# Four later modulation sections as multiply-and-sum work on VectorE, Pool and ScalarE instead of TensorE products

## The chip, the core and the metric

The kernel runs on one core of one Trainium2 chip. The metric is the device time of one execution in microseconds (us). Lower is better.

## The reference

Two requests (`prompt` and `sample`, called groups 0 and 1) go through the same two layers. Each layer begins with a modulation that is computed from the request's condition vector `c`:

```python
for l in range(DEPTH):                                   # DEPTH = 2, D_MODEL = 1024, SEQ = 512
    mod = jax.nn.silu(c) @ w_ada[l] + b_ada[l]           # (1, 1024) @ (1024, 3072)
    shift, scale, gate = jnp.split(mod, 3, axis=-1)
    h = rmsnorm(x, g_norm[l]) * (1 + scale[:, None, :]) + shift[:, None, :]
    out = even_mixer(h, ...) if l % 2 == 0 else odd_mixer(h, ...)
    x = x + gate[:, None, :] * out
return rmsnorm(x, g_final)
```

`even_mixer` starts with one input projection, `u = h @ w_in0`, whose columns go to the two kinds of attention and a SiLU gate. The modulation has six sections of 1024 values: shift, scale and gate of layer 0 and of layer 1. Shift and scale of layer 0 are needed before the first projection. The other four are needed later: the gate of layer 0 after the first output projection, those of layer 1 in the second layer.

## The kernel before

Activations lie transposed, feature by token: a tile is 128 features by T = 512 tokens, and D = 1024 is DC = 8 such tiles. One program runs a prologue (`p_*`) and then, for each group, a first layer (`a_*` is the input projection, then `b_*`, `c_*`, `d_*`) and a second layer (`e_*`). Each engine has its own hand-written sequence of instructions; they meet only through counting semaphores, and each engine works strictly in its order. All loads and stores are issued from SyncE (SP).

**The blocks.** The weights of all projections come as 81 blocks of 128 output features per group. Block b of the first in-projection (b = 0 to 24) is 8 x 3 matmuls of 128x512 (`pe_project`, `three`, L561 to L563), because each f32 operand is split into a high and a low part. For each block ScalarE makes the high half of the weights (`act_split`, L531) and VectorE the low half (`dve_split`, L543). There are PAIRS = 2 buffers of split weights and SLOTS = 3 of loaded ones (`stream_weights`, L556). ScalarE and VectorE split block b+2 in their turn b, after block b's result has been taken out of PSUM. TensorE waits for `w_lo` before each block. Block 16 is narrow (L629, 16 matmuls).

**VectorE's turn b** in `a_vector`: evict or finish block b (L832, L842, L849, L852; at b = 15 also four norms of the latents, L837), then `dve_split(b + 2)`. **Pool**, in group 0, adds masks to eight attention bias tables (L761, two instructions each) and sums the squares of the latents (L741); SP loads and stores those tables at odd b from 5. TensorE needs the sums of squares before block 9.

**The later modulation sections before.** Three passes p of TensorE compute 16 each of the 48 tiles of the modulation (6 sections x 8): pass 0 in the prologue, passes 1 and 2 in the in-projection of group 0. A pass has 8 steps, one for each 128 rows of the weights. After the block b of the table `ADA_AT` stands one `ada_step` (L303): four products of the 128x2 silu(c) with 128x512 weights, each into its own quarter of the output partitions. `ada_load` (L296) fetches the next 2 x 512 KB once the step has read the last. `ada_evict` (L319), `ada_turn` (L311, four transposes) and `ada_add` (L328) bring the sums into `mod`.

```python
ADA_AT = {b: s for s, b in enumerate((1, 3, 4, 6, 7, 9, 10, 12, 14, 15, 17, 18, 20, 21, 22, 23))}
...
for q in range(4):
    if p:
        pe.wait_ge(sem(f"ada_in{q // 2}"), 16 * (DC * (p - 1) + k + 1))
    last = pe.matmul(ps(ADA_BANK[p])[32 * q:32 * q + G], siluc[:, G * k:G * k + G], parts[q],
                     start=(k == 0), stop=(k == DC - 1))
```

After block 24 comes `b_*`, the up-projections of the latents: ScalarE takes out the first results at L947, VectorE starts at L973 after the last store of the gate (`sg_out`), Pool copies at L1004, and TensorE's first attention score is L1115.

## Time and profile before

| | |
|---|---|
| median of three runs | 1488.36 us (1488.08 to 1489.69) |
| the profiled execution, its own time | 1488.46 us |
| its span, first to last instruction | 1486.4 us |
| TensorE matmul busy | 1449.8 us, 98% of the span |
| VectorE, ScalarE, Pool busy | 854.4, 669.9, 365.2 us |
| mean granted TensorE clock | 0.997 |

The profile is one execution on the chip. "Busy" of TensorE is the union of pipelined matmuls. The in-projection of group 0 lies between 40 and 201 us of the span. The profile's chain of waits goes back from the last instruction to what released it. "Releaser" names what an engine's idle time waited for. Idle time of an engine that nobody waits for costs nothing.

### The profile page before, as it was taken

What the parts mean: (1) busy time and instruction counts of PE and PEld (TensorE: products, weight loads), DVE (VectorE), ACT (ScalarE), POOL (GpSimd) and SP (SyncE); (2) the same over time, 40 slices, a digit from 0 to 9 for tenths busy, and PEclk for the clock granted to TensorE, in tenths of its full rate; (3) what the DMA queues carried; (4) which work ended last, traced back from release to release, by engine and by line L of the source; (5) the groups of instructions that cost most, each with busy time, mean ns of one, the idle gap of its engine ahead of it and who ended that gap; (6) DMA issues with size and microseconds to landing.
All of it is one profiled execution on the core that took longest, in us unless ns stands there. A gap on an engine that the chain in (4) does not pass through costs nothing.

```text
span 1486.4 us, 18893 instructions
## 1 busy us (share of the span) xinstructions
PE 1449.8 (98%) x7162; PEld 1115.2 (75%) x7162; DVE 854.4 (57%) x1523; ACT 669.9 (45%) x1161; POOL 365.2 (25%) x455
## 2 busy tenths in 40 slices
PE   8999999999999999999999999999999999999997
PEld 5677765678787787787888887567878778787885
DVE  7523345655797427885443434566689652789423
ACT  3323446744443435543543343765444343555332
POOL 2011023421100022765210002342120002376311
PEclk9999999999999999999999999999999999999999
DMA  9566732214333331116334544222433333111531
GB/s 385 203 221 214 256 128 86 58 57 142 107 99 100 95 111 57 44 29 240 88 97 160 133 119 111 96 58 58 142 111 100 95 107 106 50 43 31 183 99 71
DMA packets 54618, 174.27 MB, mean 117 GB/s; under 512 B 6000, under 2 KB 7408, under 8 KB 52224
## 3 DMA queue, kind: packets, MB, share of 16 engines
q1 hardware_dynamic: 54528, 173.07, 36.0%
q8 instruction: 57, 0.93, 0.3%
q14 instruction: 33, 0.27, 0.1%
HBM read 149.94 MB, written 23.10 MB: 116 GB/s over the span
## 4 chain that ended last, share of the span: by engine, by line
PE 82%; DVE 8%; ACT 4%; DMA 2%; issue 2%; POOL 1%; SPq 0%; DVEq 0%; ACTq 0%; POOLq 0%
PE ps L561 21%; PE ps L563 21%; PE ps L562 21%; PE ps L1115 3%; PE ps L1151 2%; PE ps L1170 2%; PE ps L1658 1%; PE ps L1641 1%; DVE w_lo L543 1%; PE ps L303 1%; PE ps L1692 1%; PE ps L1189 1%; PE ps L1482 1%; PE ps L1132 1%; DMA at<-z_kept 1%
## 5 line engine op out<-in xcount | busy, mean ns | idle before, releaser
L543 DVE TENSOR_TENSOR w_lo<-at,w_hi 128x1024 fp32r<-128x1024 f32 x160 | 199.1, 1244 | 345.2 <-ACT w_hi L531 345.1
L531 ACT ACTIVATE w_hi<-at 128x1024 fp32r<-128x1024 f32 x162 | 169.5, 1047 | 140.1 <-PE ps L563 130.6
L561 PE MATMUL ps<-h_e_hi,w_hi 128*128 128x512 f32 x464 | 182.8, 394 | 5.0 <-DVE w_lo L543 5.0
L563 PE MATMUL ps<-h_e_hi,w_lo 128*128 128x512 f32 x464 | 180.6, 389 | 0.0
L562 PE MATMUL ps<-h_e_lo,w_hi 128*128 128x512 f32 x464 | 180.6, 389 | 0.0
L561 PE MATMUL ps<-h_a_hi,w_hi 128*128 128x512 f32 x384 | 153.7, 400 | 1.6 <-DVE h_a_lo L593 1.0
L562 PE MATMUL ps<-h_a_lo,w_hi 128*128 128x512 f32 x384 | 150.1, 391 | 0.0
L563 PE MATMUL ps<-h_a_hi,w_lo 128*128 128x512 f32 x384 | 150.0, 391 | 0.0
L561 PEld LDWEIGHTS ps<-h_e_hi,w_hi 128*128 128x128 f32 x464 | 87.1, 188 | 28.8 <-issue 8.7
L563 PEld LDWEIGHTS ps<-h_e_hi,w_lo 128*128 128x128 f32 x464 | 87.1, 188 | 18.3
L562 PEld LDWEIGHTS ps<-h_e_lo,w_hi 128*128 128x128 f32 x464 | 87.1, 188 | 18.0 <-issue 0.5
L1300 POOL TENSOR_SCALAR at<-at,at 128x256 f32<-128x256 f32 (+1 forms) x128 | 76.0, 611 | 98.9 <-DVE at L1250 98.9
L561 PE MATMUL ps<-u_h_hi,w_hi 128*128 128x512 f32 x256 | 100.2, 391 | 0.0
L563 PE MATMUL ps<-u_h_hi,w_lo 128*128 128x512 f32 x256 | 99.6, 389 | 0.0
L562 PE MATMUL ps<-u_h_lo,w_hi 128*128 128x512 f32 x256 | 99.6, 389 | 0.0
L1468 DVE SCALAR_TENSOR_TENSOR at<-ps,at,at 128x510 f32<-128x510 f32 (+1 forms) x128 | 95.9, 749 | 4.5
L561 PEld LDWEIGHTS ps<-h_a_hi,w_hi 128*128 128x128 f32 x384 | 72.4, 188 | 29.8 <-issue 12.0
L1569 POOL TENSOR_TENSOR at<-at,at 128x512 f32<-128x512 f32 x16 | 22.2, 1412 | 284.9 <-DMA at<-a_rows 284.9
L563 PEld LDWEIGHTS ps<-h_a_hi,w_lo 128*128 128x128 f32 x384 | 72.4, 188 | 15.4
L562 PEld LDWEIGHTS ps<-h_a_lo,w_hi 128*128 128x128 f32 x384 | 72.5, 189 | 14.8 <-issue 0.7
L573 POOL TENSOR_TENSOR at<-at,at 128x512 f32<-128x512 f32 x25 | 38.1, 1525 | 138.1 <-ACT at L1895 95.0
L1234 DVE TENSOR_REDUCE at<-ps 128x2 f32<-128x1024 f32 x32 | 39.2, 1225 | 42.8 <-PE ps L1115 42.8
(289 smaller groups left out, 3007.0 us busy)
## 6 DMA issues: line engine op xcount, KB each, us to landing
at<-blocks_in SPq DMA_DIRECT2D x162, 512.0 KB, 3.8
at<-w_ada SPq DMA_DIRECT2D x32, 512.0 KB, 4.6
at<-w_ada SPq DMA_DIRECT2D x8, 1024.0 KB, 17.7
at<-xs SPq DMA_DIRECT2D x4, 2048.0 KB, 10.7
z_kept<-at SPq DMA_DIRECT2D x32, 256.0 KB, 2.1
at<-z_kept SPq DMA_DIRECT2D x32, 256.0 KB, 2.7
sg_kept<-at SPq DMA_DIRECT2D x16, 256.0 KB, 4.5
at<-sg_kept SPq DMA_DIRECT2D x16, 256.0 KB, 2.6
```

The costliest lines, as they stand in the source:

```text
L531: act.activation(whi[:, n % PAIRS, :, cols], wring[:, n % SLOTS, :, cols], ACT.Copy).then_inc(sem("w_hi"), 1)
L543: dve.tensor_tensor(wlo[:, n % PAIRS], wring[:, n % SLOTS], whi[:, n % PAIRS].bitcast(F32), ALU.subtract)\
L561: pe.matmul(o, stationary[0], moving[0], start=first, stop=False)
L562: pe.matmul(o, stationary[0], moving[1], start=False, stop=False)
L563: return pe.matmul(o, stationary[1], moving[0], start=False, stop=final)
L573: pool.tensor_tensor(acc, acc, sqb[:, c % 2], ALU.add).then_inc(sem("sq_added"), 1)
L1115: last = pe.matmul(ps(s_bank(j) + e), qcat[0:QK, u, m * P:(m + 1) * P], kcat[0:QK, u], start=True, stop=True)
L1151: last = pe.transpose(ps(4 + q)[:, col:col + P], Pt[:, j % 4, m, k * P:(k + 1) * P], ident)
L1170: last = pe.matmul(ps(6 + n % 2)[64 * e:64 * e + 64, 2 * P * half:2 * P * half + 2 * P], vmla[:, s, 2 * n + e], PT[(j - 1 + e) % 4][:, 2 * ...
L1234: dve.tensor_reduce(nmx[:, 2 * i:2 * i + 2], ps2(i % 2).rearrange("p (e t) -> p e t", e=2), AX.X, ALU.max, negate=True).then_inc(sem("c_ma ...
L1300: last = pool.tensor_scalar(p, p, rinv[:, n:n + 1], 1.0, ALU.mult, ALU.mult)
L1468: dve.scalar_tensor_tensor(y[:, lo:hi], src[:, lo + d:hi + d], vb("convw", t * IC + c), y[:, lo:hi], ALU.mult, ALU.add).then_inc(sem("e_co ...
```

## The change

The four later sections leave TensorE in the in-projection of group 0. The weights of these sections are given transposed (`w_late`): a tile `w_late[t]` is 128 output features by the 1024 inputs, and `srep[g]` holds c of group g, broadcast from memory to all 128 partitions and put through SiLU once by ScalarE (both c in ScalarE's turn 0). A value of `mod` is then the sum over a row of `w_late[t] * srep[g]`.

- 24 tiles (gate of layer 0, shift and scale of layer 1) are done by VectorE, two instructions for each (`late_column`, one per group, each with a sum output), one tile in most turns b: the first instruction ahead of `dve_split`, the second behind it. None stands at b = 16, two at b = 14. Tiles 0 to 15 use two buffers in turn, tiles 16 to 23 one buffer; the load of the next waits until the last reader of its buffer is done.
- 8 tiles (gate of layer 1) are multiplied by Pool (`gate_products`, one instruction of 128x1024 per group) and summed by ScalarE (`gate_sums`) in turns b = 3, 5, ... 17; SP loads the next one (`gate_load`) after both sums of the last.
- The bias is added in `late_section` or `late_bias`. ScalarE's part of `b_*` begins with a wait for all nine increments of `mod_set`.
- The loads are 32 of 512 KB, as many bytes as before, and two of 512 KB for `srep`.
- The buffer `navT` of group 0 lies elsewhere.

```diff
-    ada_q = [take(2 * T, at=V0 + n * T) for n in (2, 9)]
+    late_w = [take(D, at=V0 + 2 * T), take(D, at=xT_lo)]
+    late_g = take(D, at=xT_lo + 2 * T)
+    late_p = take(D, at=xT_lo + 4 * T)
+    srep = [take(D, at=V0 + 9 * T), take(D, at=htmp_lo)]
+    unread = take(2 * (acc_lo - rstd_lo), at=rstd_lo).rearrange("p (h w) -> p h w", h=2)[:, :, 0:T]
...
+    LATE = 3 * DC
+    LATE_AT = [b for b in range(1, 25) for _ in range(0 if b == 16 else 2 if b == 14 else 1)]
+    ONE_SLOT = 16
+    MOD_SET = 9
...
+    def late_load(sp, t):
+
+        uses = late_uses(t)
+        if len(uses) > 1:
+            sp.wait_ge(sem("late_col"), G * (uses[-2] + 1))
+        sp.dma_start(late_w[late_slot(t)], w_late[t]).then_inc(sem(f"ada_in{late_slot(t)}"), 16)
+
+    def late_column(dve, t, g):
+
+        if g == 0:
+            dve.wait_ge(sem(f"ada_in{late_slot(t)}"), 16 * (1 + len(late_uses(t))))
+        if t == 0:
+            dve.wait_ge(sem("p_silu"), g + 2)
+        if t or g:
+            dve.wait_ge(sem("late_col"), G * t + g)
+        l, c = divmod(2 * DC + t, 3 * DC)
+        w = late_w[late_slot(t)].rearrange("p (h w) -> p h w", h=2)
+        dve.scalar_tensor_tensor(w if g else unread, w, 1.0, srep[g].rearrange("p (h w) -> p h w", h=2), ALU.mult, ALU.mult,
+                                 accum_out=mod[:, l, c, g:g + 1]).then_inc(sem("late_col"), 1)
...
+    def gate_load(sp, k):
+
+        if k:
+            sp.wait_ge(sem("late_sum"), G * k)
+        sp.dma_start(late_g, w_late[LATE + k]).then_inc(sem("ada_in2"), 16)
+
+    def gate_products(pool, k):
+
+        if k == 0:
+            pool.wait_ge(sem("p_silu"), 1 + G)
+        pool.wait_ge(sem("ada_in2"), 16 * (k + 2))
+        if k:
+            pool.wait_ge(sem("late_sum"), G * k)
+        for g in range(G):
+            if g:
+                pool.wait_ge(sem("late_prod"), G * k + g)
+            pool.tensor_tensor(late_g if g else late_p, late_g, srep[g], ALU.mult).then_inc(sem("late_prod"), 1)
+
+    def gate_sums(act, k):
+
+        for g in range(G):
+            act.wait_ge(sem("late_prod"), G * k + g + 1)
+            o = late_g if g else late_p
+            act.activation(o, o, ACT.Copy, accum_out=mod[:, 1, 2 * DC + k, g:g + 1]).then_inc(sem("late_sum"), 1)
...
-        ada_load(sp, 0)
+        sp.wait_ge(sem("ada_used"), 4)
+        late_load(sp, 0)
+        sp.dma_start(srep[0], c_in[0:1, :].to_broadcast([P, D])).then_inc(sem("ada_in3"), 16)
...
-                if g == 0 and b in ADA_AT and ADA_AT[b] + 1 < ADA_STEPS:
-                    ada_load(sp, ADA_AT[b] + 1)
+                if g == 0:
+                    for t in range(1, LATE):
+                        if max(LATE_AT[t] - 1, 1) == b:
+                            if t == 1:
+                                sp.wait_ge(sem("h_lo"), DC)
+                                sp.dma_start(srep[1], c_in[1:2, :].to_broadcast([P, D])).then_inc(sem("ada_in4"), 16)
+                            late_load(sp, t)
+                    if b % 2 and b // 2 < DC:
+                        gate_load(sp, b // 2)
                 stream_weights(sp, b + 1)
...
+            for k in range(2):
+                gate_products(pool, k)
...
+                if h + 2 < DC:
+                    gate_products(pool, h + 2)
+            pool.wait_ge(sem("late_sum"), G * DC)
+            late_bias(pool, 1, 2 * DC)
...
-                if g == 0:
-                    if b in ADA_AT:
-                        ada_step(pe, 1 + ADA_AT[b] // DC, ADA_AT[b] % DC,
-                                 [ada_q[q // 2][:, q % 2 * T:(q % 2 + 1) * T] for q in range(4)])
-                    if b == B_NAV + 1:
-                        pe.wait_ge(sem("lat_ln"), at("lat_ln", 2))
-                        ada_turn(pe, 1)
-                    if b == B_OUT0 - 1:
-                        ada_turn(pe, 2)
...
+                todo = [t for t in range(LATE) if LATE_AT[t] == b] if g == 0 else []
+                for t in todo[:1]:
+                    late_column(dve, t, 0)
                 dve_split(dve, b + PAIRS)
+                for t in todo:
+                    if t > todo[0]:
+                        late_column(dve, t, 0)
+                    late_column(dve, t, 1)
+                    if (t + 1) % DC == 0:
+                        late_section(dve, t)
...
+                if g == 0 and b == 0:
+                    for n in range(G):
+                        act.wait_ge(sem(f"ada_in{3 + n}"), 32)
+                        act.activation(srep[n], srep[n], ACT.Silu).then_inc(sem("p_silu"), 1)
+                if g == 0 and b >= 3 and b % 2 and (b - 3) // 2 < DC:
+                    gate_sums(act, (b - 3) // 2)
...
-                            act.wait_ge(sem("h_scaled"), DC)
+                            act.wait_ge(sem("late_col"), G * ONE_SLOT)
                         act.wait_ge(sem("lat_ready"), at("lat_ready", 4))
+                    if g == 0 and b == B_GATE + 1:
+                        act.wait_ge(sem("late_sum"), G * DC)
...
         def b_scalar(act):
+            if g == 0:
+                act.wait_ge(sem("mod_set"), MOD_SET)```

The order on ScalarE around turns 0 to 3 of the in-projection, before (`at_3072_66` is the ring of loaded weights, `at_2048_81` the latents):

```order
L898 ACTIVATE at_2048_81<-ps 128x512 [waits blk_done]
L531 ACTIVATE w_hi<-at_3072_66 128x1024 [waits blk_done,w_in2]
L531 ACTIVATE w_hi<-at_3072_66 128x1024 [waits blk_done,w_in0]
L898 ACTIVATE at_2048_81<-ps 128x512 [waits blk_done]
L531 ACTIVATE w_hi<-at_3072_66 128x1024 [waits blk_done,w_in1]
L531 ACTIVATE w_hi<-at_3072_66 128x1024 [waits blk_done,w_in2]
```

and in the changed kernel, where `at_1024_120` and `at_1024_121` are `srep[0]` and `srep[1]`, and `at_1024_119` and `at_1024_118` are `late_p` and `late_g`:

```order
L963 ACTIVATE at_2048_81<-ps 128x512 [waits blk_done]
L590 ACTIVATE w_hi<-at_3072_66 128x1024 [waits blk_done,w_in2]
L991 ACT_TABLE_LOAD
L991 ACTIVATE at_1024_120<-at_1024_120 128x1024 [waits ada_in3]
L991 ACTIVATE at_1024_121<-at_1024_121 128x1024 [waits ada_in4]
L590 ACTIVATE w_hi<-at_3072_66 128x1024 [waits blk_done,w_in0]
L963 ACTIVATE at_2048_81<-ps 128x512 [waits blk_done]
L590 ACTIVATE w_hi<-at_3072_66 128x1024 [waits blk_done,w_in1]
L590 ACTIVATE w_hi<-at_3072_66 128x1024 [waits blk_done,w_in2]
L362 ACTIVATE at_1024_119,at_96_52<-at_1024_119 128x1024 [waits late_prod]
L362 ACTIVATE at_1024_118,at_96_52<-at_1024_118 128x1024 [waits late_prod]
```

The two SiLUs stand between the splits of blocks 2 and 3; the second waits for the load of `srep[1]`.

The order on SP at its turn 1, in the changed kernel (`at_1024_121` is `srep[1]`, `at_1024_117` and `at_1024_116` the two buffers of VectorE's tiles, `at_1024_118` Pool's buffer):

```order
L759 DMA at_1536_79<-up_q 128x1536 [waits p_fold]
L760 DMA at_2048_82<-up_kv 128x2048
L787 DMA at_1024_121<-c_in 128x1024 [waits h_lo]
L302 DMA at_1024_117<-w_late 128x1024
L343 DMA at_1024_118<-w_late 128x1024
L615 DMA at_3072_66<-blocks_in 128x1024 [waits w_lo]
```

Before, two loads of `w_ada` stood at the place of the three from `c_in` and `w_late`.

The order on VectorE in turn 4, before:

```order
L849 SCALAR_TENSOR_TENSOR naq_lo<-ps,naq_hi 128x128 [waits naqk_hi]
L849 SCALAR_TENSOR_TENSOR naq_lo<-ps,naq_hi 128x128 x2
L849 SCALAR_TENSOR_TENSOR naq_lo<-ps,naq_hi 128x8x8 x2
L543 TENSOR_TENSOR w_lo<-at_3072_66,w_hi 128x1024 [waits w_hi]
```

and in the changed kernel (`at_96_52` is `mod`, `at_15360_122` the output that nobody reads):

```order
L914 SCALAR_TENSOR_TENSOR naq_lo<-ps,naq_hi 128x128 [waits naqk_hi]
L914 SCALAR_TENSOR_TENSOR naq_lo<-ps,naq_hi 128x128 x2
L914 SCALAR_TENSOR_TENSOR naq_lo<-ps,naq_hi 128x8x8 x2
L314 SCALAR_TENSOR_TENSOR at_15360_122,at_96_52<-at_1024_117,at_1024_120 128x2x512 [waits late_col,ada_in1]
L602 TENSOR_TENSOR w_lo<-at_3072_66,w_hi 128x1024 [waits w_hi]
L314 SCALAR_TENSOR_TENSOR at_1024_117,at_96_52<-at_1024_117,at_1024_121 128x1024 [waits late_col]
```

One instruction over two tiles of SBUF now stands on either side of the split.

## Rows read from the trace of the kernel before

**Rows 1.** The page: busy us (share of the span) x instructions.
```profile
PE 1449.8 (98%) x7162; PEld 1115.2 (75%) x7162; DVE 854.4 (57%) x1523; ACT 669.9 (45%) x1161; POOL 365.2 (25%) x455
```
**Rows 2.** Busy us, blocks 3 to 16: PE, PEld, DVE, ACT, POOL; clock, DMA share, GB/s.
```profile
59.50:148.80 89.30, 89.30 (x427) 63.86 (x425) 28.55 (x47) 26.59 (x41) 11.51 (x14) 1.00 0.68 231
```
**Rows 3.** Timeline of TensorE: start us, us, operation [idle before <-releaser].
```profile
64.57 0.39 PE L562 MATMUL ps<-h_a_lo,w_hi 128*128 128x512 f32 x1
64.80 0.39 PE L563 MATMUL ps<-h_a_hi,w_lo 128*128 128x512 f32 x1
65.12 1.04 PE L303 MATMUL ps<-at,at 128*2 128x512 f32 x8
...
66.43 0.40 PE L562 MATMUL ps<-h_a_lo,w_hi 128*128 128x512 f32 x1
```
**Rows 4.** The same timeline: the steps or turns that are not like that.
```profile
54.06 0.47 PE L561 MATMUL ps<-h_a_hi,w_hi 128*128 128x512 f32 x1 [0.65 <-DVE w_lo L543]
...
71.75 1.31 PE L303 MATMUL ps<-at,at 128*2 128x512 f32 x8
...
186.39 2.17 PE L303 MATMUL ps<-at,at 128*2 128x512 f32 x8
...
200.70 0.60 PE L311 MATMUL ps<-at,at 128*128 128x128 f32 x4
```
**Rows 5.** DMA issues between 54.6 and 56.3 us: KB each, median us to landing.
```profile
at<-up_kv SPq DMA_DIRECT2D x1, 1024.0 KB, 7.2
at<-w_ada SPq DMA_DIRECT2D x2, 512.0 KB, 8.4
```
**Rows 6.** Timeline of SP: when those loads of `w_ada` were issued.
```profile
55.26 1.03 SPq L296 DMA_DIRECT2D at<-w_ada  x2
```
**Rows 7.** Timeline of VectorE and Pool where both use two tiles of SBUF.
```profile
328.10 0.75 DVE L1356 SCALAR_TENSOR_TENSOR y_e_lo<-at,at,y_e_hi 128x512 fp32r<-128x512 f32 x1
328.14 1.86 POOL L573 TENSOR_TENSOR at<-at,at 128x512 f32<-128x512 f32 x1 [3.58 <-ACT at L1369]
333.54 1.87 DVE L1356 SCALAR_TENSOR_TENSOR y_e_lo<-at,at,y_e_hi 128x512 fp32r<-128x512 f32 x1
333.58 1.29 POOL L573 TENSOR_TENSOR at<-at,at 128x512 f32<-128x512 f32 x1 [3.58 <-ACT at L1369]
```
**Rows 8.** Groups by line and shape: names, shapes xcount | busy us, mean ns.
```profile
L1966 DVE DVE_READ_ACCUMULATOR at<-ps,at 128x1 f32 x64 | 5.2, 82 | 0.0
L531 ACT ACTIVATE w_hi<-at 128x1024 fp32r<-128x1024 f32 x162 | 169.5, 1047 | 140.1 <-PE ps L563 130.6
L543 DVE TENSOR_TENSOR w_lo<-at,w_hi 128x1024 fp32r<-128x1024 f32 x13 | 16.1, 1242 | 12.3 <-ACT w_hi L531 12.3
L837 DVE SCALAR_TENSOR_TENSOR at<-at,at,at 128x512 f32<-128x512 f32 x4 | 2.7, 744 | 0.0
L741 POOL TENSOR_TENSOR at<-at 128x512 f32<-128x512 f32 x2 | 2.5, 1280 | 0.0
L761 POOL TENSOR_TENSOR at<-at,at 128x256 f32<-128x256 f32 x16 | 12.1, 775 | 133.5 <-DMA t_masked<-at 77.9 <-DMA at<-rpb_pad 55.6
```
**Rows 9.** DMA issues at 81 us: one load of a block alone in the queue.
```profile
at<-blocks_in SPq DMA_DIRECT2D x1, 512.0 KB, 3.5
```
**Rows 10.** Stretch behind the prologue (clock 0.50), and TensorE's timeline there.
```profile
40.00:41.00 1.00, 1.00 (x3) 0.70 (x3) 1.00 (x2) 0.00 (x0) 0.00 (x0) 0.50 0.78 320
...
39.61 0.76 PE L561 MATMUL ps<-h_a_hi,w_hi 128*128 128x512 f32 x1 [0.98 <-DVE h_a_lo L593]
...
42.31 0.45 PE L561 MATMUL ps<-h_a_hi,w_hi 128*128 128x512 f32 x1
```
**Rows 11.** Timeline behind block 24 (started at 195.12): VectorE, Pool, TensorE.
```profile
208.61 0.68 DVE L973 TENSOR_TENSOR at<-ps,at 32x512 f32<-32x512 f32 x1 [4.54 <-DMA sg_kept<-at]
211.84 5.78 POOL L1004 COPY at<-at 32x512 f32<-32x512 f32 x7 [0.68 <-DVE at L977]
220.72 1.88 PE L1115 MATMUL ps<-at,at 96*128 96x512 f32 x4
```

More of the change, by code:

```diff
@@ L81, in out1_block, with trunk @@
     return 4 * quad + n % 4, n // 4
-def trunk(nc, xs, rows_in, fold_in, w_ada, blocks_in, up_q, up_kv, rpb_pad, const_in, out):
+def trunk(nc, xs, rows_in, c_in, fold_in, w_ada, w_late, blocks_in, up_q, up_kv, rpb_pad, const_in, out):
     a_rows = nc.dram_tensor("a_rows", (2 * ML_H, T), F32, kind="Internal").ap()
@@ L392, in p_tensor @@
         for k in range(DC):
[L393 to L394 removed]
+            pe.wait_ge(sem(f"ada_in{k}"), 16)
+            ada_step(pe, k)
             if k == 5:
@@ L2268 @@
     out = nc.dram_tensor("out", (G, D, T), F32, kind="ExternalOutput").ap()
-    trunk(nc, t["xs"], t["rows_in"], t["fold_in"], t["w_ada"], t["blocks_in"], t["up_q"], t["up_kv"], t["rpb_pad"], t["const_in"], out)
+    trunk(nc, t["xs"], t["rows_in"], t["c_in"], t["fold_in"], t["w_ada"], t["w_late"], t["blocks_in"], t["up_q"], t["up_kv"], t["rpb_pad"], t["const_in"], out)
     r = run_bass_kernel_spmd(nc, [arrays], core_ids=[0])
```

109 lines of the change are left out of this document (50 added, 59 removed).

## The prediction

> **What bounds the kernel now.** I read the page first: TensorE is busy for 98% of the span [rows 1]. So what leaves TensorE is worth its full price, provided that nothing makes TensorE wait. The busy time by stretch says the same of the place of the change: from block 3 to block 16 TensorE is busy for all of 89.3 us, at full clock (2.4 GHz), while VectorE has 28.55 us of work, ScalarE 26.59 and Pool 11.51 [rows 2]. By busy time alone there is room for all that is moved. What has to be asked is when each piece runs and what waits behind it.
>
> **What is removed.** The timeline of TensorE shows the price of one step. In a block, matmuls start every 0.23 us (64.57, 64.80). Around a step the last L563 starts at 64.80 and the second matmul of the next block at 66.43, 1.63 us where two intervals are 0.45: a step costs 1.18 us [rows 3]. There are 16, but the one behind block 1 is free: block 2 then still waits 0.65 us for `w_lo` [rows 4], and will without it. 15 x 1.18 = 17.7. Two steps took longer for their weights: 1.31 us where others take 1.04, which is 0.3 more, and 2.17, 1.1 more [rows 3, 4]. The last turn took 0.5 (L311 at 200.70, 0.60 long, with the next product started at 201.23), and the other about as much. Sum removed: 17.7 + 0.3 + 1.1 + 1.0 = **20.1 us**.
>
> **The second SiLU, in front of the split of block 3.** ScalarE cannot split block 3 before `srep[1]` is there. SP issues that load in its turn 1 behind `up_q` and `up_kv`, where the first `w_ada` load went out at 55.26 [rows 6]. `up_kv`, issued at 54.8, landed after 7.2 us, and the two `w_ada` loads behind it after 8.4 in the median [rows 5], so `srep[1]` lands near 63.6. Then come the SiLU (1.05, taken from L531, which has its shape), the high half (1.05) and the low half (1.24) [rows 8]: block 3 starts at 67.0. It started at 59.5 before [rows 2]. Nothing stands in between that TensorE could do. **+7.5 us.** Between 4 (the load overtakes part of `up_kv`) and 9 (128 reads of one row are slow).
>
> **VectorE and Pool, blocks 3 to 16.** The timeline shows that the two exclude each other when both work on two tiles of SBUF. A Pool product of 512 takes 1.29 us alone, and 1.86 when VectorE's L1356 had begun 0.04 us earlier; the same L1356 takes 0.75, and 1.87 when Pool got in first [rows 7]. Each time the loser waits for the winner's whole instruction (0.75 - 0.18, and 1.29 - 0.17). The Trainium skill (SBUF — State Buffer, SBUF: two separate sides) calls it an exclusive lock held for a whole instruction, which speaks against putting such work on both engines at once; the trace agrees (0.57 and 1.12 us of waiting). New instructions of this kind are 48 columns on VectorE and 16 products on Pool. What needs the pair between the starts of block 3 and block 17 [rows 8]:
> - 16 Pool products of 1024, two of 512 each: L741's two took 2.5, so 16 x 2.5 = 40.0
> - 31 columns (tiles 0 to 15, less the very first) at the price of L543, 1.24: 38.4
> - 13 splits of full width 16.1, the narrow one about 0.4
> - 14 of L761's 16, each of half a 512 at 0.64: 9.0; its mean of 775 ns includes waiting
> - L741 2.5, L837 2.7.
>
> That is 109 us. TensorE's own work there is 89.3 less nine steps (10.6), less 0.3 and 0.5: 78.0. The pair is asked for 31 us more than TensorE needs. The last tile's two products (5 us) may fall behind block 17, and the pair stands idle while Pool waits for a load and VectorE for ScalarE. These two about cancel. **+30 us**, from 15 (if much of Pool's work slips into the later blocks) to 40 (if the idle time is larger: each round of Pool is load, two products, two sums, and SP, on which the block loads hang too, waits for the sums). Where the stall shows: TensorE waits for `w_lo`, because a product stands before a split or a column.
>
> **One buffer, blocks 17 to 24.** From tile 17 on the load waits for the last reader. A round is: landing of 512 KB 3.5 [rows 9] with 0.1 to issue, two columns and one split 3 x 1.24, two reads of the sum 0.08 each [rows 8]: 7.5 us. A block is 24 x 0.227 = 5.4. So from where VectorE's slack of some 3 us is used up, each block waits 2.1. The slack lasts until block 20, and the last two tiles hold no block of this projection. Blocks 21 to 24 wait: 4 x 2.1, less what is left of the slack, **+7.5** (4 to 12; the store of the gate and the block loads can delay a landing).
>
> **Behind block 24.** VectorE ends the last section some 16.6 us after block 24 starts, since tiles 22 and 23 each need another round. ScalarE waits for it before its first eviction. In the kernel before, Pool's copies, before the first score, ended at 217.6, and the score started at 220.7, so 3 us of slack lie there. VectorE's start hangs on the last store [rows 11], which now goes out behind the split of block 26, near 19.2 us after the start of block 24 where it was 13.5 (208.61 less 195.12), 5.7 later. 5.7 less 3 gives **+3** (1 to 7).
>
> **Clock.** Behind the prologue's small matmuls the granted clock was 0.50, that is 1.2 GHz, and six matmuls took 2.70 us (39.61 to 42.31) in place of 1.36 [rows 10]. No row shows a gap in full blocks, so each of the gaps (one of 7.5 us, some eight of 2 to 7) costs between 0 and 1.35; part of it is covered, since the pair and not TensorE sets the end. **+3** (0 to 10). The Trainium skill, TensorE: Matmul & The Clock Gate, Why this matters for your kernels, says to avoid idle gaps in the middle of a kernel for this reason; by it nearly every long gap would cost the full 1.35, and the sum would be about 5 us higher.
>
> ScalarE's sums (16 of some 1.2 us) and its wait for Pool are inside the third term. The loads carry the same bytes: no term.
>
> **Sum.** -20.1 + 7.5 + 30 + 7.5 + 3 + 3 = +30.9 on the execution's 1488.46, 1519.4. The median is 0.1 lower: **1519 us**. Its own range is 1503 to 1534.
>
> **The rivals.**
> - *The pair costs about half*: Pool's products run mostly while VectorE evicts from PSUM or waits. For: VectorE is idle for long in the trace of before. Against: the sum of 109 counts only what excludes. The third term is 10 to 15: about 1502.
> - *The round of Pool is the longer one*: load 3.5, two products 5, waits for the lock up to 2 x 1.24, two sums 2.4, with SP's block loads behind it: 13.4 for two blocks (10.9), and VectorE waits on top. The third term is 50: 1540.
> - *The pair costs nothing*, and the two loops and the SiLU remain: -20.1 + 7.5 + 7.5 + 3 + 1.4 = -0.7, 1488. Rows 7 are against it.
> - *Faster*: the work hides as its busy time suggests. The mechanism is that TensorE gets its 20.1 us back because VectorE always has the low half ready. It needs no exclusion, and a round of the single buffer under 5.4 us, that is a landing under 1.5 us in place of 3.5. Then only the SiLU (7.5) and 2 are left: 1478. Against it: rows 7 and 9.
>
> **Chances.** My forecast 0.70, half the pair's cost 0.10, the longer round 0.10, no cost of the pair 0.05, faster 0.05. The range of 1500 to 1535 holds the forecast's own range and most of the half-cost case. About 0.2% (3 us) is what a measurement of this kernel can tell from no change. Faster by more than that 0.05, within it 0.05, slower 0.90.
>
> **What would show it.** In the profile after: no L303 after 50 us; TensorE's wait before block 3 near 7.5 us, released by the split; Pool products of 2.5 us alone and up to 3.7 behind VectorE, with splits and columns stretched up to 3.7; TensorE waiting for `w_lo` between blocks 4 and 17 for about 30 us in all; block starts 7.5 us apart from block 20; VectorE waiting for `w_late` there; stretches at clock 0.50 in the in-projection. I am wrong if products and columns keep their short durations side by side, or if block 3 starts before 63 us.

## The result, and the profile after

The changed kernel takes **1519.18 us** (median of four runs, 1515.15 to 1519.66), the one before 1488.44 (1488.08 to 1489.69): ratio 1.0197, with a 95% interval of 1.0184 to 1.0209. It is 30.7 us slower. The forecast was 1519. The profiled execution took 1519.66, its span is 1517.8.

The busy line of the page of the changed kernel, which answers to [rows 1]:

```profile
PE 1446.2 (95%) x7026; PEld 1120.8 (74%) x7026; DVE 942.8 (62%) x1618; ACT 689.4 (45%) x1196; POOL 421.7 (28%) x472
```

TensorE has 136 matmuls fewer and is busy for only 3.6 us less, since part of them runs at the lower clock. VectorE gained 88 us of busy time and Pool 56, for work that takes some 59 and 40 us at the lone prices of [rows 7, 8]. (A lone price is what an instruction takes when the other engine is idle.)

The waits of TensorE in the in-projection of the changed kernel, in its timeline (start us, us, operation, idle time in front and who ended it):

```profile
66.76 0.79 PE L620 MATMUL ps<-h_a_hi,w_hi 128*128 128x512 f32 x1 [7.07 <-DVE w_lo L602]
92.93 0.47 PE L620 MATMUL ps<-h_a_hi,w_hi 128*128 128x512 f32 x1 [1.57 <-DVE w_lo L602]
101.86 0.47 PE L620 MATMUL ps<-h_a_hi,w_hi 128*128 128x512 f32 x1 [3.22 <-DVE w_lo L602]
...
163.38 1.09 PE L847 MATMUL ps<-at,at 128*128 128x128 f32 x4 [6.27 <-DVE at L907]
165.61 0.79 PE L620 MATMUL ps<-h_a_hi,w_hi 128*128 128x512 f32 x1 [1.14 <-DVE w_lo L602]
192.50 0.47 PE L620 MATMUL ps<-h_a_hi,w_hi 128*128 128x512 f32 x1 [2.26 <-DVE w_lo L602]
200.00 0.47 PE L620 MATMUL ps<-h_a_hi,w_hi 128*128 128x512 f32 x1 [1.80 <-DVE w_lo L602]
207.44 0.47 PE L620 MATMUL ps<-h_a_hi,w_hi 128*128 128x512 f32 x1 [1.75 <-DVE w_lo L602]
214.81 0.47 PE L620 MATMUL ps<-h_a_hi,w_hi 128*128 128x512 f32 x1 [1.69 <-DVE w_lo L602]
...
231.99 1.47 PE L1098 MATMUL ps<-at,at 128*128 128x512 f32 x2 [2.06 <-ACT at L1022]
```

The first row is block 3 behind the second SiLU. The next ones, with two smaller ones left out, are the pair, VectorE and Pool holding each other up. At 163.38 the token transposes in front of block 17 wait 6.3 us for one eviction of VectorE. The last four block rows are blocks 21 to 24, 7.4 to 7.5 us apart, where a block is 5.44 us of work.

Why that eviction is late stands in the timelines of VectorE and Pool of the changed kernel:

```profile
154.88 7.80 DVE L902 SCALAR_TENSOR_TENSOR at<-at,at,at 128x512 f32<-128x512 f32 x4
162.60 0.68 DVE L907 COPY at<-ps 128x512 f32<-128x512 f32 x1
...
153.78 6.19 POOL L355 TENSOR_TENSOR at<-at,at 128x1024 f32<-128x1024 f32 x2 [4.43 <-DMA at<-w_late]
159.94 2.20 POOL L831 TENSOR_TENSOR at<-at,at 128x256 f32<-128x256 f32 x2
```

Four norms that take 2.7 us alone [rows 8] take 7.80 beside two products and a mask of Pool, and the copy that TensorE needs is queued behind them. Pool's products stretch too: 6.19 for two that take 5.0 alone. This is the exclusion of [rows 7], in the place where it costs most.

The same stretches by engine, in columns as in [rows 2]: blocks 3 to 16, blocks 17 to 23, and from block 24 to the first score.

```profile
66.76:165.61 98.85, 84.74 (x348) 66.07 (x348) 93.75 (x107) 43.03 (x71) 61.79 (x29) 0.93 0.64 208
165.61:214.81 49.20, 41.70 (x168) 33.16 (x169) 33.11 (x41) 17.84 (x27) 8.97 (x7) 0.94 0.58 187
214.81:246.16 31.35, 27.96 (x102) 20.09 (x103) 19.51 (x28) 10.06 (x17) 8.27 (x9) 0.89 0.37 116
```

VectorE is busy for 93.75 of 98.85 us between block 3 and block 17, where it had 28.55 of 89.3 before [rows 2]. Waiting for Pool counts as busy in such a row: an engine that looks full may be one that is locked out. By line and shape, in the same stretch:

```profile
L355 POOL TENSOR_TENSOR at<-at,at 128x1024 f32<-128x1024 f32 x15 | 44.5, 2965 | 66.2 <-DMA at<-w_late 65.6
L314 DVE SCALAR_TENSOR_TENSOR at<-at,at 128x1024 f32<-128x1024 f32 x31 | 60.9, 1965 | 0.9 <-DMA at<-w_late 0.5
L602 DVE TENSOR_TENSOR w_lo<-at,w_hi 128x1024 fp32r<-128x1024 f32 x13 | 22.7, 1747 | 0.6 <-ACT w_hi L590 0.6
```

A product takes 2.97 us in the mean, a column 1.97 and a split 1.75; the splits took 1.24 before [rows 8].

Where the 31 us are, by starts that the timelines of TensorE show (us from the span's start; each run is told of below):

| kernel | block 3 | block 17 | block 24 | first score | span |
|---|---|---|---|---|---|
| before | 59.5 | 148.8 | 195.1 | 220.7 | 1486.4 |
| changed | 66.8 | 165.6 | 214.8 | 246.2 | 1517.8 |
| e1, SiLU moved | 60.2 | 161.6 | 211.0 | 242.3 | 1514.9 |
| e2, no products on Pool | 67.1 | 147.9 | 196.7 | 227.8 | 1496.0 |
| e3, products half as wide | 67.4 | 153.7 | 202.8 | 234.9 | 1503.7 |
| e4, narrow columns | 67.6 | 152.3 | 200.1 | 231.9 | 1500.6 |
| e5, copies on Pool | 67.1 | 152.1 | 201.4 | 234.0 | 1500.8 |
| e6, short tail | 67.4 | 165.0 | 207.0 | 233.3 | 1503.0 |
| e7, three out | 63.2 | 147.1 | 186.1 | 213.3 | 1483.0 |
| e8, before, fewer steps | 59.9 | 139.4 | 177.6 | 203.0 | 1468.4 |
| e9, half and half | 62.9 | 147.3 | 200.4 | 225.9 | 1492.0 |
| e10, later second tile | 60.1 | 148.8 | 203.7 | 229.3 | 1495.3 |
| e11, changed, once more | 67.4 | 169.6 | 218.0 | 249.3 | 1520.5 |
| e12, spread steps | 59.9 | 147.4 | 190.5 | 216.2 | 1481.6 |

The offset to the kernel before grows to 7.3 us at block 3, 16.8 at block 17, 19.7 at block 24 and 25.4 at the first score. The last 6 arise in the attention of both groups, where nothing was changed.

### The profile page after: what moved, and what is told of

The parts are those of the page before. It is cut to its first block, busy times and chain, and to the rows that moved or that the text cites. A ratio compares the mean times of both kernels' runs of the same rounds, so it can differ in the third digit from the quotient of the medians.

```text
span 1517.8 us, 18800 instructions
## 1 busy us (share of the span) xinstructions
PE 1446.2 (95%) x7026; PEld 1120.8 (74%) x7026; DVE 942.8 (62%) x1618; ACT 689.4 (45%) x1196; POOL 421.7 (28%) x472
## 4 chain that ended last, share of the span: by engine, by line
PE 73%; DVE 13%; DMA 5%; ACT 4%; issue 2%; POOL 1%; SPq 0%; DVEq 0%; ACTq 0%; POOLq 0%
PE ps L620 19%; PE ps L622 18%; PE ps L621 18%; PE ps L1187 4%; DVE w_lo L602 3%; DVE at L314 3%; DMA at<-w_late 2%; PE ps L1223 2%; PE ps L1242 2%; PE ps L1730 1%; PE ps L1713 1%; PE ps L1764 1%; ACT w_hi L590 1%; PE ps L1261 1%; PE ps L1554 1%
## 5 line engine op out<-in xcount | busy, mean ns | idle before, releaser
L602 DVE TENSOR_TENSOR w_lo<-at,w_hi 128x1024 fp32r<-128x1024 f32 x160 | 205.6, 1285 | 305.2 <-ACT w_hi L590 305.1
L590 ACT ACTIVATE w_hi<-at 128x1024 fp32r<-128x1024 f32 x162 | 169.6, 1047 | 140.7 <-PE ps L622 131.4
L620 PE MATMUL ps<-h_e_hi,w_hi 128*128 128x512 f32 x464 | 182.8, 394 | 4.8 <-DVE w_lo L602 4.8
L620 PE MATMUL ps<-h_a_hi,w_hi 128*128 128x512 f32 x384 | 155.7, 406 | 25.5 <-DVE w_lo L602 24.0
L620 PEld LDWEIGHTS ps<-h_a_hi,w_hi 128*128 128x128 f32 x384 | 73.8, 192 | 48.2 <-issue 21.1
L620 PEld LDWEIGHTS ps<-h_e_hi,w_hi 128*128 128x128 f32 x464 | 87.1, 188 | 28.5 <-issue 8.4
L620 PE MATMUL ps<-u_h_hi,w_hi 128*128 128x512 f32 x256 | 100.2, 391 | 0.0
L314 DVE SCALAR_TENSOR_TENSOR at<-at,at 128x1024 f32<-128x1024 f32 x48 | 81.7, 1701 | 23.4 <-DMA at<-w_late 22.4
## 6 DMA issues: line engine op xcount, KB each, us to landing
at<-blocks_in SPq DMA_DIRECT2D x162, 512.0 KB, 3.7
at<-w_late SPq DMA_DIRECT2D x32, 512.0 KB, 4.4
at<-w_ada SPq DMA_DIRECT2D x8, 1024.0 KB, 17.9
```

Of the source, the lines that this page charges most:

```text
L314: dve.scalar_tensor_tensor(w if g else unread, w, 1.0, srep[g].rearrange("p (h w) -> p h w", h=2), ALU.mult, ALU.mult, accum_out=mod[:, l, ...
L590: act.activation(whi[:, n % PAIRS, :, cols], wring[:, n % SLOTS, :, cols], ACT.Copy).then_inc(sem("w_hi"), 1)
L602: dve.tensor_tensor(wlo[:, n % PAIRS], wring[:, n % SLOTS], whi[:, n % PAIRS].bitcast(F32), ALU.subtract)\
L620: pe.matmul(o, stationary[0], moving[0], start=first, stop=False)
```

## The experiments

e2 to e8 were run once each. The changed kernel's eight runs (its four and those of e11) lie between 1515.15 and 1522.29 us, and its two profiles differ by 3.4 us in the stretch from block 3 to block 17. Differences of that size between two single runs say little.

**What left TensorE: e8.** In the kernel before, the later two passes do one of their eight steps each (the other seven, and their loads, are left out):

```diff
-                if g == 0 and b in ADA_AT and ADA_AT[b] + 1 < ADA_STEPS:
-                    ada_load(sp, ADA_AT[b] + 1)
+                if g == 0 and b in ADA_AT and ADA_AT[b] == DC - 1:
+                    ada_load(sp, DC)
...
-                    if b in ADA_AT:
+                    if b in ADA_AT and ADA_AT[b] % DC == 0:
```

> The kernel before with one step in place of eight in each of its two later passes on TensorE (14 steps and 14 pairs of loads are left out, nothing takes their place). It measures what the removed products were worth. My price: 14 x 1.18 and 1.4 for two longer ones: -17.9, 1470.5 (1469 to 1472). Rival, the steps lay partly in time in which TensorE would have waited anyway: 1478 or more.

Measured: 1470.46 us, 18.0 less than the 1488.44 of before. The price of 1.18 us a step holds on the whole program, and nothing waits in the place of the steps.

**The second SiLU: e1.** The load of `srep[1]` goes ahead of the up weights in SP's turn 1, and its SiLU into ScalarE's turn 1. Nothing is left out. The part on ScalarE:

```diff
-                if g == 0 and b == 0:
-                    for n in range(G):
-                        act.wait_ge(sem(f"ada_in{3 + n}"), 32)
-                        act.activation(srep[n], srep[n], ACT.Silu).then_inc(sem("p_silu"), 1)
+                if g == 0 and b < G:
+                    act.wait_ge(sem(f"ada_in{3 + b}"), 32)
+                    act.activation(srep[b], srep[b], ACT.Silu).then_inc(sem("p_silu"), 1)
```

> The load of srep[1] is issued first in SP's turn 1, and the second SiLU stands behind the split of block 3. Nothing is left out. If block 3 waits for that SiLU (7.3 us between 59.5 and 66.8 in the changed kernel), it now starts at 59.5 to 61 and the time falls by 6 to 8 us, to about 1512. Rival: the wait is only passed on, because the first columns and Pool's first products are bound to the same load: block 3 starts on time, but blocks 4 to 6 wait instead and less than 3 us is gained.

Measured: 1514.81 us, ratio to before 1.0192 (1.0134 to 1.0250). The changed kernel's ratio lies inside this interval, so the four runs do not show a gain in the total. That block 3 waited for the SiLU is shown by the start of block 3, at 60.2 and 6.6 us earlier than in the changed kernel. What became of these 6.6 us is less clear: 6.4 are left at block 4, 4.1 at block 5, 4.0 at block 17 and 2.9 at the end, but against the second profile of the changed kernel (e11) 8.0 are left at block 17. Neither of the two expected outcomes came as it was written: the gain is 2.9 us by the spans and 4.4 by the medians. The timeline of its TensorE:

```profile
68.44 0.77 PE L620 MATMUL ps<-h_a_hi,w_hi 128*128 128x512 f32 x1 [2.65 <-DVE w_lo L602]
...
82.72 0.47 PE L620 MATMUL ps<-h_a_hi,w_hi 128*128 128x512 f32 x1 [0.77 <-DVE w_lo L602]
89.75 0.47 PE L620 MATMUL ps<-h_a_hi,w_hi 128*128 128x512 f32 x1 [1.35 <-DVE w_lo L602]
97.96 0.47 PE L620 MATMUL ps<-h_a_hi,w_hi 128*128 128x512 f32 x1 [2.49 <-DVE w_lo L602]
```

The first row is block 4, which did not wait in the changed kernel. This wait of 2.65 us, the lower clock in block 4 (0.80) and a wait of 0.6 before block 5 stand against a block 3 at the lower clock in the changed kernel (0.66, 8.1 us for 5.44 of work); together they take 2.5 of the 6.6 us away. Why block 4 waits stands at e7. From block 5 to block 17 this profile and the first one of the changed kernel both take 85.3 us, and e11 88.8.

**Exclusion or too much work: e2 to e5.** Each leaves the order, the loads and the waits as they are and shortens one of the two sides. In e2 and e3 Pool multiplies only 8 or 512 columns of each tile (all but the very first product; the rest of the last section is left out):

```diff
-            pool.tensor_tensor(late_g if g else late_p, late_g, srep[g], ALU.mult).then_inc(sem("late_prod"), 1)
+            o = late_g if g else late_p
+            n = D if k == g == 0 else 8
+            pool.tensor_tensor(o[:, 0:n], late_g[:, 0:n], srep[g][:, 0:n], ALU.mult).then_inc(sem("late_prod"), 1)
```

> Pool's products are 8 columns wide except the very first (the last modulation section is left out but for that). If VectorE and Pool exclude each other over SBUF, blocks 3 to 17 take some 80 us instead of 98.9 and the time falls by 16 to 20 us, to about 1501; columns and splits keep 1.22 us. If lower clock or VectorE's own load sets the stalls there, less than 8 us is gained.

Measured: 1497.75 us, 21.4 less than the changed kernel and somewhat more than expected.

> Pool's products are 512 wide except the very first (half of the last section is left out). Demand for the shared access falls by 15 x 1.25 = 19 us, from 109 to 90, where TensorE needs 78. Exclusion as a sum over the whole stretch forecasts 12 us of stall and so 8 to 10 us less than the changed kernel. If what counts is whether one product fits into a gap of VectorE, the gain is nearly that of e2.

Measured: 1505.52 us, 13.7 less. That lies between the 8 to 10 of the sum over the stretch and the 21.4 of e2, so neither form of the theory gives it: half of the products' width gives back more than half of what all of it costs.

In e4 it is the other side: VectorE's columns of tiles 0 to 15 sum 8 elements (the rest of these sums is left out), and Pool's products stay whole.

```diff
+        n = 4 if t < ONE_SLOT else T
-        dve.scalar_tensor_tensor(w if g else unread, w, 1.0, srep[g].rearrange("p (h w) -> p h w", h=2), ALU.mult, ALU.mult,
+        dve.scalar_tensor_tensor((w if g else unread)[:, :, 0:n], w[:, :, 0:n], 1.0,
+                                 srep[g].rearrange("p (h w) -> p h w", h=2)[:, :, 0:n], ALU.mult, ALU.mult,
```

> VectorE's columns of tiles 0 to 15 are 2 x 4 wide (two sections are left out), Pool's products stay whole. Exclusion: demand is 109 - 38 = 71, under TensorE's 78, so blocks 3 to 17 take about 80 us and the time falls by 15 to 20 us. Rival, the round of Pool's load, two products and ScalarE's two sums with SP behind it (about 12 to 13 us for two blocks of 10.9): it needs no column, so most of the stall stays and less than 8 us is gained.

Measured: 1502.35 us, 16.8 less, with Pool's products whole; the stretch takes 84.7 us, where about 80 was expected. So the longer round of Pool does not set the end. Both sides are cheap alone and dear together; that is what the theory says and what a plain shortage of time on one engine would not give. The stretch between the starts of blocks 3 and 17, by engine, first in e4 and then in e2:

```profile
67.61:152.27 84.66, 81.16 (x349) 64.30 (x349) 56.57 (x108) 40.93 (x69) 48.89 (x28) 0.97 0.72 237
```

```profile
67.06:147.91 80.85, 79.71 (x349) 64.17 (x349) 66.39 (x107) 40.82 (x70) 29.22 (x27) 0.98 0.77 251
```

With the products gone, VectorE's busy time falls from 93.75 to 66.39 us, though its own work is the same: at least 27 us of it was waiting. TensorE's stretch is 80.85, where its work is 78.0. In e4 a column of 8 elements takes 0.15 us where Pool is idle and 2.35 where a product has just begun, and 0.76 in the mean, since it waits for whole products (from the timelines, and by line and shape):

```profile
73.33 0.15 DVE L315 SCALAR_TENSOR_TENSOR at<-at,at 128x8 f32<-128x8 f32 x1
119.13 2.35 DVE L315 SCALAR_TENSOR_TENSOR at<-at,at 128x8 f32<-128x8 f32 x1
...
119.01 2.45 POOL L357 TENSOR_TENSOR at<-at,at 128x1024 f32<-128x1024 f32 x1 [4.07 <-DMA at<-w_late]
...
L315 DVE SCALAR_TENSOR_TENSOR at<-at,at 128x8 f32<-128x8 f32 x31 | 23.5, 759 | 5.6 <-DMA at<-w_late 5.4
```

In e5 Pool copies 1024 columns in place of each product (the multiplication is left out):

```diff
-            pool.tensor_tensor(late_g if g else late_p, late_g, srep[g], ALU.mult).then_inc(sem("late_prod"), 1)
+            pool.tensor_copy(late_p if g == 0 else late_g, late_g if g == 0 else srep[g]).then_inc(sem("late_prod"), 1)
```

> Pool copies 128x1024 (one input) where it multiplied two (the multiplication of the last section's elements is left out; the loads, the order and ScalarE's sums stay). Pool's L1558 of before, 128x512 with one input, takes 0.71 us where two inputs take 1.28, so a copy should take 1.4 where a product took 2.5, close to the products of half width. Theory that VectorE's two-input instructions and any instruction of Pool exclude each other: as with the half products, block 17 starts near 154 and the time is near 1505. Rival, only Pool instructions with two inputs exclude: as with no products, block 17 starts near 148 and the time is 1498.

Measured: 1502.58 us, with block 17 at 152.1: between the two, and nearer to the half products by the start of block 17 (153.7, against 147.9 without products). The copies took 1.56 us each in the mean, and columns and splits of VectorE are stretched beside them, as its timelines show:

```profile
81.57 3.02 POOL L355 COPY at<-at 128x1024 f32<-128x1024 f32 x2 [11.67 <-DMA at<-w_late]
83.62 2.04 DVE L602 TENSOR_TENSOR w_lo<-at,w_hi 128x1024 fp32r<-128x1024 f32 x1
88.73 1.21 DVE L602 TENSOR_TENSOR w_lo<-at,w_hi 128x1024 fp32r<-128x1024 f32 x1
```

The split takes 2.04 us beside the copies and 1.21 where Pool is idle: an instruction of Pool with one input excludes too, which I had left open. Against e2 block 17 starts 4.2 us later. The Trainium skill, SBUF — State Buffer, Who interferes with whom, puts the condition on Pool's side at reading SBUF at all, and the trace agrees. The time by itself, between the two expected ones, would not have told the theories apart.

**The single buffer and what lies behind block 24: e6.** Tiles 17 to 23 are loaded and summed at half width (half of each of these sums is left out).

```diff
-        sp.dma_start(late_w[late_slot(t)], w_late[t]).then_inc(sem(f"ada_in{late_slot(t)}"), 16)
+        n = T if t > ONE_SLOT else D
+        sp.dma_start(late_w[late_slot(t)][:, 0:n], w_late[t][:, 0:n]).then_inc(sem(f"ada_in{late_slot(t)}"), 16)
```

> Tiles 17 to 23 are loaded and summed at half width (half of each of those sums is left out). Theory of the single buffer: a round is then a landing near 2 us and three instructions of VectorE of which two are half as long, under 5.4 us; the four waits of 1.7 to 2.3 us before blocks 21 to 24 go (-7.5), and VectorE ends the last section before TensorE needs its next bank behind block 24, so of the 7.4 us behind it some 4 go: 1508 (1505 to 1511). Rival, what follows block 24 hangs on the later store and not on the last section: only the 7.5 go, 1512. Rival, the loads are late for their number and not for their size: 1519.

Measured: 1504.82 us, 14.4 less, just under the expected range. From block 17 to block 24 it takes 42.0 us in place of 49.2, and from there to the first score 26.3 in place of 31.4. Both expected parts came, 7.2 and 5.0 us, and the other 2 us lie ahead of block 17 and behind the first score. The rounds of the changed kernel that this took away are plain in the timeline of its VectorE:

```profile
204.92 1.22 DVE L314 SCALAR_TENSOR_TENSOR at<-at,at 128x1024 f32<-128x1024 f32 x1 [2.19 <-DMA at<-w_late]
...
212.29 1.22 DVE L314 SCALAR_TENSOR_TENSOR at<-at,at 128x1024 f32<-128x1024 f32 x1 [2.12 <-DMA at<-w_late]
...
219.78 1.23 DVE L314 SCALAR_TENSOR_TENSOR at<-at,at 128x1024 f32<-128x1024 f32 x1 [3.97 <-DMA at<-w_late]
...
227.30 1.23 DVE L314 SCALAR_TENSOR_TENSOR at<-at,at 128x1024 f32<-128x1024 f32 x1 [4.01 <-DMA at<-w_late]
...
234.74 0.68 DVE L1047 TENSOR_TENSOR at<-ps,at 32x512 f32<-32x512 f32 x1 [3.44 <-DMA sg_kept<-at]
```

Each round is a load, two columns and a split, 7.4 to 7.5 us apart to the end: the two last tiles have no block over them and run bare.

**All three together: e7** (the same parts left out as in e2 and e6, SiLU as in e1).

> The SiLU moved, Pool's products 8 wide and the last seven tiles at half width, together (the last section and half of tiles 17 to 23 are left out). Theory that nothing but these three and the clock behind their gaps stands between what left TensorE and the time: 1519.2 - 6.6 (block 3) - 18.9 (blocks 3 to 16) - 8 (17 to 24) - 5 (behind 24) - 3 (clock in the attention) = 1478, and no more than 1481. Rival, another part of the change costs too (ScalarE's sums, the extra loads, VectorE's 48 columns beside the work it had): 1484 or more, with TensorE waiting between blocks 4 and 24.

Measured: 1484.8 us, inside the rival's range. Of it 3.4 us lie ahead of all this: block 0 started at 43.2 where it starts between 39.3 and 39.9 in e1 to e6. Some 0.7 of them came from a load of `w_ada` in the prologue; the rest arose between 26 and 34 us, where TensorE ran at half clock. Here are three microseconds of it in e7, and the same three in the changed kernel (columns: stretch, TensorE's busy time, clock, DMA share, GB/s):

```profile
28.00:31.00 3.00, 3.00 (x12) 0.50 0.99 407
```

```profile
28.00:31.00 3.00, 3.00 (x23) 1.00 1.00 404
```

Nothing was changed in the prologue. Without that I estimate 1481.4. TensorE waited 2.57 us before block 4, where the timeline of VectorE shows a column that stood in front of the split and waited for its tile:

```profile
68.88 1.22 DVE L316 SCALAR_TENSOR_TENSOR at<-at,at 128x1024 f32<-128x1024 f32 x1 [3.47 <-DMA at<-w_late]
70.03 0.08 DVE L316 DVE_READ_ACCUMULATOR at<-at,at 128x1 f32 x1
70.03 1.22 DVE L607 TENSOR_TENSOR w_lo<-at,w_hi 128x1024 fp32r<-128x1024 f32 x1
```

So a fourth part, small, was not in the account: the load of the second tile goes out with the up weights and lands late. It had been hidden by the wait for the SiLU, and it is the wait before block 4 of e1 too.

**A split of the work that keeps Pool out: e9, e10, e12.** All three compute everything. 16 columns' tiles (the gate of layer 0, the shift of layer 1) are on VectorE behind blocks 1 to 14, in two buffers; scale and gate of layer 1 stay one pass of eight steps on TensorE; Pool and ScalarE get nothing. Their edits on the changed kernel, cut to the places:

```diff
-    LATE_AT = [b for b in range(1, 25) for _ in range(0 if b == 16 else 2 if b == 14 else 1)]
+    LATE_AT = [b for b in range(1, 15) for _ in range(2 if b in (12, 14) else 1)]
+    STEP_AT = 16
...
+                if g == 0 and STEP_AT <= b < STEP_AT + DC:
+                    ada_step(pe, 1, b - STEP_AT)
```

> The whole computation, split differently: 16 column tiles (the gate of layer 0 and the shift of layer 1) on VectorE behind blocks 1 to 14, with two of them behind 12 and 14; scale and gate of layer 1 as one pass on TensorE, a step behind each of the blocks 16 to 23. Nothing on Pool and ScalarE, two buffers throughout, the second SiLU in ScalarE's next turn. From the kernel before: seven steps and a turn fewer, 7 x 1.18 + 0.5 + 0.3 = -9.1 (-10.2 with the long step). My theory (only the pair, the SiLU and the single buffer made the change slow): 1480, plus what the late second tile costs in front of block 4 (2.6 us in the two runs that moved the SiLU) and the clock behind it: 1482 to 1484. Rival, 32 two-input instructions of VectorE behind 14 blocks are too many of themselves: waits before blocks 12 to 15, 1488 or more.

Measured: 1495.36 us, ratio 1.0042 (1.0018 to 1.0067): slower than before, a miss by 12 us. Neither the theory nor its rival fits: no block from 12 to 15 waited. In its profile block 0 started 3.3 us late, as in e7 and at the same half clock in the prologue (0.50 from 28 to 31 us), the step behind block 16 waited 1.2, and from block 17 to block 24 it took 53.0 us, 6.7 more than seven blocks and seven steps at 5.44 and 1.18. e10 changes one line of it (here against e9):

```diff
-    LATE_AT = [b for b in range(1, 15) for _ in range(2 if b in (12, 14) else 1)]
+    LATE_AT = [b for b in range(1, 15) if b != 2 for _ in range(2 if b in (9, 11, 13) else 1)]
```

> As e9, but no tile behind block 2 and doubles behind blocks 9, 11 and 13, so that the second tile's load is issued one turn later and read two blocks after that of the first, and the block loads go ahead of it. Theory (the split of block 4 stood behind a column whose load landed late): TensorE's wait of 2.6 us before block 4 and the half clock behind it go: 1480 (1478 to 1481.5). Rival (the loads around the two up weights are late in whatever order): block 4 or 5 still waits, and the time is that of e9.

Measured: 1498.15 us, ratio 1.0052 (1.0034 to 1.0071), another miss. The wait before block 4 did go: blocks 3 to 10 follow each other without one, with a column tile behind nearly each. But doubles behind blocks 11 and 13 held blocks 12 and 14 up by 0.91 and 2.04 us. And both kernels lose more behind block 16 (in e10 8.5 us between blocks 17 and 24), as the timelines of TensorE show, here of e9, whose rows are steps:

```profile
160.07 1.43 PE L353 MATMUL ps<-at,at 128*2 128x512 f32 x8
167.10 2.02 PE L353 MATMUL ps<-at,at 128*2 128x512 f32 x8
174.71 1.77 PE L353 MATMUL ps<-at,at 128*2 128x512 f32 x8
182.08 1.97 PE L353 MATMUL ps<-at,at 128*2 128x512 f32 x8
...
199.39 1.03 PE L353 MATMUL ps<-at,at 128*2 128x512 f32 x4 [1.53 <-DMA at<-w_tail]
```

They are 7.0 to 7.6 us apart, where a step and a block took 6.62 before. Eight steps behind eight blocks, each with 1 MB to load beside a block's 0.5 MB and the stores, come faster than the loads: these landed after 5.3 us in the median. The kernel before had gaps in its table of steps, and I had kept the number of steps and lost the gaps.

e12 spreads the steps, loads them up to two blocks ahead, and puts the doubles behind 9, 12 and 14. The matmuls of the latent means go to banks 4 and 6, so that bank 5 is free for the pass from block 10 on; early steps are loaded into what was `late_g` and `late_p`. The lines against e9:

```diff
-    LATE_AT = [b for b in range(1, 15) for _ in range(2 if b in (12, 14) else 1)]
-    STEP_AT = 16
+    LATE_AT = [b for b in range(1, 15) if b != 2 for _ in range(2 if b in (9, 12, 14) else 1)]
+    STEP_AT = (10, 12, 14, 16, 18, 20, 22, 23)
+    STEP_LOAD = (8, 10, 12, 15, 16, 18, 20, 22)
```

> The whole computation. As e9 and e10, with both of their losses addressed. Columns: 16 tiles on VectorE, none behind block 2 (in e9 the second tile's late load kept block 4 waiting), doubles behind 9, 12 and 14 (in e10 the doubles behind 11 and 13 kept blocks 12 and 14 waiting 0.9 and 2.0 us, those of e9 behind 12 and 14 nobody). Steps of the one remaining pass behind blocks 10, 12, 14, 16, 18, 20, 22 and 23 in place of 16 to 23, with their loads up to two blocks ahead (in e9 and e10 the blocks with a step took 7.0 to 9.2 us where those of the kernel before took 6.62). Theory (VectorE's columns alone hide, and e9 and e10 lost their gain to loads that came too close): from the kernel before seven steps, a turn and the longer steps: 1479 (1477 to 1482). Rival (the load of 24.7 MB where 22 were moved is itself too much between blocks 3 and 16): TensorE waits at the steps behind 10, 12 and 14, and the time is 1485 or more.

Measured: **1484.75 us**, ratio 0.9979 (0.9970 to 0.9988), over 11 runs: 3 to 4 us faster than the kernel before and 34 faster than the changed one, and the only complete version here that beats both. The expected 1479 it missed: it lies 0.3 us under the rival's 1485, and of the waits that the rival names it has those behind blocks 14 and 16. The timeline of its TensorE says where part of the loss is:

```profile
105.52 1.26 PE L354 MATMUL ps<-at,at 128*2 128x512 f32 x8
...
131.83 1.03 PE L354 MATMUL ps<-at,at 128*2 128x512 f32 x4 [0.24 <-DMA at<-w_tail]
...
144.78 1.03 PE L354 MATMUL ps<-at,at 128*2 128x512 f32 x4 [1.72 <-DMA at<-w_tail]
...
158.49 1.04 PE L354 MATMUL ps<-at,at 128*2 128x512 f32 x8
```

From the step behind block 18 on the loads are in time (1.04 in the row shown), though a load of `w_tail` lands after 5.0 us in the median, hardly sooner than the 5.3 of e9: what changed is the time that a step leaves it. The two steps behind blocks 14 and 16, whose loads share the queue with the tiles of the last doubles, still waited 2.2 us in all. The rest of the 6 us was not followed.

**The changed kernel once more: e11.**

> The changed kernel once more, to see what the clock does in the attention. In its first profile 5.8 us of the 31.2 arose behind the first scores (the clock was 0.89 to 0.95 where it was 1.00 before), in e1 6.7, in the runs with a faster in-projection only 2.3 to 3.8. If that is tied to this kernel, it shows again, and the time is 1519. If it varies from run to run, some run of it is near 1515, as one of the four was, and the part behind the first scores is 2 to 4 us.

Measured: 1517.43 us (1516.77 to 1522.29), ratio 1.0189 (1.0149 to 1.0229). In its profile 1271.2 us lie behind the first score's start, where it was 1271.6 in the first one and 1265.7 before. So the 6 us in the attention came again, and no run of it was near 1515: that fits the first expected outcome, a cost tied to this kernel.

## Why the prediction was right, point by point

- **What is removed, 20.1.** Right. e8 gave back 18.0 for 14 steps that I price at 17.9.
- **The second SiLU, 7.5.** Right as a place and a size: block 3 started at 66.76, predicted 67.0, and the wait was 7.07. What it cost the whole is open: with the SiLU moved 2.9 to 4.4 us came back, no more than the runs of one kernel differ by, and 2.5 of the 6.6 us went in blocks 3 and 4, since the second tile was late. That wait stands behind the SiLU's, and the forecast does not name it.
- **VectorE and Pool, 30.** Mechanism right, size too large: the stretch took 98.85 us against 78.0 of TensorE's work, 20.9 (24.2 in e11's profile). The forecast's demand of 109 fails in two places. Of Pool's work one product and two of the small sums fell behind block 17, 3.8 us by my prices, where I had taken this slip to cancel against idle time. The rest, 105, still does not fit into 98.85: added up from the two timelines, Pool or a two-input instruction of VectorE is running for only 91.9 us of the stretch. Lone durations overlap when instructions follow each other: in [rows 7] the two take 1.90 and 1.87 us end to end where their lone times add up to 2.04, and a column and the split behind it start 1.15 us apart where each lasts 1.22 (e7). How much each kind of overlap is worth was not measured. The sign that I had named came in part: TensorE waited for `w_lo` between blocks 4 and 17 not for 30 us but for 6.7, with 1.1 more before block 17 and 6.3 for the late eviction, 14.1 in all; the other 6.8 of the 20.9 are slower matmuls. By its size the term lies about midway between my 30 and the 10 to 15 of the rival of half the cost. That rival's mechanism, products that run while VectorE evicts or waits, is not what happened: VectorE was busy for 93.75 of the 98.85 us. The rival of Pool's round falls by e4: with the products whole and the columns narrow the stretch takes 84.66 us. e2 puts the price of the products at 18.0 us in this stretch.
- **The lock.** The Trainium skill, SBUF — State Buffer, SBUF: two separate sides, says that it is held for a whole instruction, whichever engine came first. The trace agrees; e4's column of 8 elements, 2.35 us behind a product that had begun 0.12 us earlier and 0.15 alone, is the clearest row for that.
- **One buffer, 7.5.** Right: the four waits are 2.26, 1.80, 1.75 and 1.69, together 7.5, in the blocks named, at the round of 7.5 that was worked out.
- **Behind block 24, 3.** Too small. It is 6.3: 31.35 us to the first score where there were 25.6, of which the turn, 0.5, had been removed (the 7.4 in the text of e6 takes off the step behind block 23 as well, which lies ahead of block 24). The times were right: the last section ended 16.5 us behind the start of block 24 (16.6 forecast), and VectorE began 19.9 behind it (19.2). The step that failed is what I let TensorE lose by them, only VectorE's delay less a slack of 3 us. TensorE's own wait for ScalarE, which waited for the section, I had put at nothing. It was 2.06 and 1.34 us (L1098), and the clock was 0.79 over the last 16 us. e6 took 5.0 of it away with nothing but shorter rounds.
- **Clock, 3.** In the in-projection right in kind, too small in size: 0.93 in blocks 3 to 16 and 0.94 behind them. The slower matmuls are 6.8 us of the first stretch. How much of that TensorE would otherwise have spent waiting, no run shows. Not foreseen was the attention, below: some 6 us in both profiles.
- **The sum.** -20.1, +7.5, +30, +7.5, +3 and +3 stand against what the same stretches measure: -20.1 (11.3 before block 17, 8.3 behind it, 0.5 behind block 24), +7.3, +20.9, +11.1 from block 17 to 24 (49.2 against seven blocks of 5.44; 7.5 of it are the four waits, the rest is mostly the half clock behind the long wait at 163.38), +6.3, and +5.9 in the attention: +31.4 of span. The right total came from a pair term that was 9 too large and terms for the tail and the clock that were together about as much too small. That the two errors cancel is luck; the places and the mechanisms are not.

## What to carry to other kernels

Ask of two engines not only whether each has time, but whether their instructions can run beside each other: here VectorE had 60 us to spare and Pool 78. VectorE's share alone hid but for 3 us (e2), and the two together cost 21. A wait can hide the one behind it: with the SiLU moved block 3 started 6.6 us earlier and block 4 waited 2.6 us for a late tile (e1, e7, e9), so look at what the next block needs before a wait is priced at its length. And when steps with loads are moved, move their spacing with them: a table of places is also a rate at which the DMA has to deliver, which cost e9 and e10 most of their gain and e12 a part of it.
